# Two decoder blocks on one core: the delta rule's inverse in 32x32 blocks with VectorE's transposes, and gate projections in column tiles

## The reference, cut to what matters

```python
def gdn_mixer(h, w_in, w_conv, a_log, dt_bias, w_onorm, w_out):
    proj = h @ w_in
    qkv, z, beta_logit, a_logit = jnp.split(proj, [3 * GDN_WIDTH, 4 * GDN_WIDTH, 4 * GDN_WIDTH + H], axis=-1)
    qkv = jax.nn.silu(causal_conv(qkv, w_conv))          # 4 taps
    q = q * lax.rsqrt(jnp.sum(q * q, -1) + EPS) / sqrt(d); k = k * lax.rsqrt(jnp.sum(k * k, -1) + EPS)
    ...
# per head and chunk
L = jnp.where(strict, k_beta @ k.T * decay, 0.0)
T = inverse(eye + L)                                     # unit lower triangular
u = T @ v_beta
w = T @ (k_beta * jnp.exp(g_cum))
# scan over chunks
v_new = u_c - w_c @ state
o = qd @ state + qk_c @ v_new
state = state * jnp.exp(gl) + kd.T @ v_new
```

## Time and profile before

| | |
|---|---|
| median of 3 executions | 2048.74 us (2048.35 to 2049.61) |
| the profiled execution | 2048.42 us |
| its span, first to last instruction | 2046.6 us |
| TensorE / VectorE / ScalarE / GpSimd busy | 98% / 72% / 28% / 17% |
| granted TensorE clock, mean | 0.997 |

### The profile page before, as it was taken

The page is one execution under the profiler, slowest core; times in us unless marked ns, Lnnn a source line. Parts: engine busy times, 40 slices in busy tenths (PEclk is TensorE's granted clock), DMA queues, the critical chain, the costliest instruction groups (busy, mean ns, idle before and its releaser), DMA issues.

```text
span 2046.6 us, 31786 instructions
## 1 busy us (share of the span) xinstructions
PE 2015.8 (98%) x12910; PEld 1619.7 (79%) x12910; DVE 1464.6 (72%) x2281; ACT 569.0 (28%) x994; POOL 352.9 (17%) x320
## 2 busy tenths in 40 slices
PE   8999999999999999999999999999999999999999
PEld 6888788887777777777788877777888888888887
DVE  5766666668877777667898887576666778849973
ACT  2000122222544444324883233434310010000000
POOL 2212111111101010012111211111121212222221
PEclk9999999999999999999999999999999999999999
DMA  4323222222211121122222332111223332322232
GB/s 163 112 93 103 80 89 91 93 83 76 84 57 60 63 69 58 64 73 78 68 69 74 119 108 78 62 52 47 78 84 97 100 101 93 104 92 96 101 98 88
DMA packets 53362, 173.73 MB, mean 85 GB/s; under 512 B 6337, under 2 KB 6721, under 8 KB 53089
## 3 DMA queue, kind: packets, MB, share of 16 engines
q1 hardware_dynamic: 48112, 161.67, 23.8%
q10 hardware_dynamic: 5104, 10.03, 1.7%
HBM read 169.51 MB, written 2.16 MB: 84 GB/s over the span
## 4 chain that ended last, share of the span: by engine, by line
PE 45%; DVE 7%; ACT 1%; issue 1%; DVEq 0%; ACTq 0%
PE ps_lin L1818 13%; PE ps_lin L1820 13%; PE ps_lin L1819 13%; PE ps_att L1864 3%; DVE arena L409 2%; PE ps_aux L1864 1%; DVE w_lo L409 1%; ACT arena L1270 1%; DVE arena L415 1%; DVE arena L897 1%; DVE y_lo L409 0%; PE ps_att L1873 0%; DVE sq L409 0%; DVE xw_lo L415 0%; DVE x L409 0%
## 5 line engine op out<-in xcount | busy, mean ns | idle before, releaser
L1818 PE MATMUL ps_lin<-xw_hi,w_hi 128*128 128x512 f32 (+1 forms) x1728 | 698.4, 404 | 0.0
L1820 PE MATMUL ps_lin<-xw_hi,w_lo 128*128 128x512 f32 (+1 forms) x1728 | 674.9, 391 | 0.0
L1819 PE MATMUL ps_lin<-xw_lo,w_hi 128*128 128x512 f32 (+1 forms) x1728 | 674.0, 390 | 0.0
L391 POOL TENSOR_SCALAR w_hi<-raw 128x1024 fp32r<-128x1024 f32 (+5 forms) x312 | 348.3, 1117 | 1678.3 <-PE ps_lin L1820 1554.4
L409 DVE TENSOR_TENSOR w_lo<-raw,w_hi 128x1024 fp32r<-128x1024 f32 (+2 forms) x344 | 381.2, 1111 | 47.9 <-POOL w_hi L391 17.5
L1270 ACT ACTIVATE arena<-arena 128x512 f32<-128x512 f32 (+7 forms) x331 | 206.4, 631 | 742.7 <-DVE arena L409 365.7
L1820 PEld LDWEIGHTS ps_lin<-xw_hi,w_lo 128*128 128x128 f32 (+1 forms) x1728 | 322.7, 187 | 71.6
L1818 PEld LDWEIGHTS ps_lin<-xw_hi,w_hi 128*128 128x128 f32 (+1 forms) x1728 | 323.0, 187 | 68.8 <-issue 4.0
L1819 PEld LDWEIGHTS ps_lin<-xw_lo,w_hi 128*128 128x128 f32 (+1 forms) x1728 | 323.5, 187 | 61.0
L409 DVE TENSOR_TENSOR arena<-ps_lin,rstd 128x512 f32<-128x512 f32 (+2 forms) x213 | 146.7, 689 | 200.5 <-PE ps_lin L1820 185.9
L1818 PE MATMUL ps_lin<-y_hi,w_hi 128*128 128x512 f32 (+1 forms) x544 | 205.4, 378 | 1.2 <-DVE w_lo L409 1.1
(11 more groups left out here) (175 smaller groups left out, 1693.1 us busy)
## 6 DMA issues: line engine op xcount, KB each, us to landing
raw<-in_w_up SPq DMA_DIRECT2D x44, 512.0 KB, 3.3
raw<-in_conv_w_in SPq DMA_DIRECT2D x32, 512.0 KB, 3.3
raw<-in_fox_w_in SPq DMA_DIRECT2D x32, 512.0 KB, 3.3
raw<-in_gdn_w_in SPq DMA_DIRECT2D x32, 512.0 KB, 3.3
raw<-in_w_gate SPq DMA_DIRECT2D x24, 512.0 KB, 3.2
raw<-in_swa_w_in SPq DMA_DIRECT2D x20, 512.0 KB, 3.2
raw<-in_w_ml SPq DMA_DIRECT2D x16, 512.0 KB, 3.3
raw<-in_w_down SPq DMA_DIRECT2D x16, 512.0 KB, 3.5
```

The costliest lines, as they stand in the source:

```text
L391: pool.tensor_scalar(w_whole(n, kc * c)[0], w_raw(n, kc * c), 1.0, 0.0, mult, add).then_inc(s("w_rounded"), 1)
L1818: pe.matmul(o, wh, hi, start=first and k == 0, stop=False)
L1819: pe.matmul(o, wh, lo, start=False, stop=False)
L1820: ins = pe.matmul(o, wl, hi, start=False, stop=last and k == kc - 1)
```

## The change

1. **Gate tiles.** GpSimd skips gate units. VectorE multiplies the raw weights by the norm's weights into `gate_w`, and TensorE multiplies them in plain fp32 with `x` itself, in four column tiles at 0, 32, 64 and 96: for Fox four groups of 128 tokens, for the other two layers two sets of outputs times two halves of 256 tokens. `gate_rows` evacuates each with its own instruction.
2. **The inverse** runs to 32x32 in levels 1 to 4, in `Uc` alone: VectorE copies `V` into `Uc`, and its transpose of 32x32 blocks makes `Ts` from it. The second group loses the product `Y` there, and the first transpose and its copy by ScalarE go. Level 5 joins two 32x32 blocks to 64x64, with 32x32 tiles: `Y` stays only for the upper triangle (`Th`); ScalarE puts the blocks into `Th` and `U`, eight copies. Level 6 is as before.
3. **The fillers** of VectorE come from tables of its own, `DVE_FILL` (before and behind the second group's work of a level) and `DVE_SCAN_FILL`; the four steps ahead of level 1 go to later places. `LEVEL_FILL` of level 3 is 2 instead of 1, in place of the chunk behind the first transpose. Pieces of the last round move by a place.
4. **The first tap** of the convolution is ScalarE's: right behind the evacuation of query and key, three steps later for value.

```diff
-        LEVEL_FILL = (0, 2, 2, 1, 1, 2, 1)
+        LEVEL_FILL = (0, 2, 2, 2, 1, 2, 1)
+        DVE_FILL = (None, (1, 2), (1, 4), (1, 1), (1, 0), (1, 2), (1, 1))
+        DVE_SCAN_FILL = (1, 1, 2, 3)
...
+        def gate_tiles(w, c):
+
+            if w == "fox_w_f":
+                return [(0, c, 32 * j, slice(j * P, (j + 1) * P)) for j in range(NT)]
+            return [(i * c // 2, c // 2, 64 * j + 32 * i, slice(j * T // 2, (j + 1) * T // 2)) for j in range(2) for i in range(2)]
...
+            def gate_rows(t, w, dst, first, release):
+
+                n, c = LAST_UNIT[t], UNITS[LAST_UNIT[t]][4]
+                for col0, m, at, tokens in gate_tiles(w, c):
+                    if col0 == first:
+                        size = tokens.stop - tokens.start
+                        last = tt(dst[:, tokens], ps_lin[at:at + m, t % BANKS, 0:size], rstd[at:at + m, tokens], mult)
...
@@ VectorE, gdn_tile
-                if n:
-                    dve.wait_ge(s("gdn_silu"), n)
-                step(ts(F["t"], F["u"][:, 3:3 + T], col("gdn_w_conv", 3 * 24 + j), mult))
                 for k in range(3):
                     yield
+                    if k == 0:
+                        dve.wait_ge(s("gdn_tap"), n + 1)
...
@@ VectorE, gdn_head
                 U0 = chunks(F["Uc"])
-                for top in (0, HD):
-                    step(tt(U0[top:top + HD], chunks(F["LT"])[top:top + HD, :, top:top + HD], over_chunks(mat("pairs0_ident")[top:top + HD, 0:HD], HD), mult))
-                tt(U0, U0, over_chunks(mat("pairs0_ident")[:, HD:]), add).then_inc(s("gdn_U0"), 1)
+                for at in range(0, P, SQ):
+                    last = tt(U0[at:at + SQ], chunks(F["LT"])[at:at + SQ, :, at:at + SQ], over_chunks(mat("pairs")[at:at + SQ, 0:SQ], SQ), mult)
+                step(last)
+                step(tt(U0, U0, over_chunks(mat("pairs")[:, SQ:2 * SQ]), add))
+                dve.transpose(F["Ts"], F["Uc"]).then_inc(s("gdn_T0"), 1)
...
-                fill(GDN_FILL["U0"])
-                fill(1)
...
-                    fill(1)
+                    fill(DVE_FILL[l][0])
                     if l < 6:
-                        dve.wait_ge(s("gdn_TX"), 5 * h + l)
-                        tt(part(F["Tm"]), part(F["Tm"]), ps_att[:, 1, 0:P].rearrange("p (b d) -> p b d", d=d), add).then_inc(s("gdn_T"), 1)
+                        if l < 5:
+                            dve.wait_ge(s("gdn_XU"), 6 * h + l)
+                            step(dve.tensor_copy(part(F["Uc"], 1), new(ps_att[:, 3, :])))
+                            dve.transpose(F["Ts"], F["Uc"]).then_inc(s("gdn_T"), 1)
+                        else:
+                            dve.wait_ge(s("gdn_TX"), h + 1)
+                            dve.tensor_copy(chunks(F["Th"])[SQ:, :, 0:SQ], chunks(ps_att[SQ:HD, 1, 0:NT * SQ])).then_inc(s("gdn_T"), 1)
...
-                    fill(LEVEL_FILL[l])
+                    fill(DVE_FILL[l][1])
...
-                    fill(1)
+                    fill(DVE_SCAN_FILL[c])
...
@@ ScalarE, gdn_tile
+                def tap():
+
+                    t, n, j = tile_of("gdn_w_in", part * 8 + r), 3 * r + part, part * 8 + r
+                    act.wait_ge(bank_read(t), reads(t))
+                    activation(F["t"], F["u"][:, 3:3 + T], ACT.Copy, scale=col("gdn_w_conv", 3 * 24 + j)).then_inc(s("gdn_tap"), 1)
+
+                late = part == 2 and r
+                if not late:
+                    tap()
...
@@ ScalarE, gdn_head
-                act.wait_ge(s("gdn_U0T"), h + 1)
-                activation(F["Tm"][:, 0:NT * HD], ps_att[:, 2, 0:NT * HD], ACT.Copy).then_inc(s("gdn_T0"), 1)
...
                     if l == 5:
-                        act.wait_ge(s("gdn_U"), 7 * h + 5)
-                        activation(U[0:HD, :, 0:HD], Uc[0:HD], ACT.Copy)
-                        activation(U[HD:, :, HD:], Uc[HD:], ACT.Copy).then_inc(s("gdn_U"), 1)
+                        act.wait_ge(s("gdn_T"), 5 * h + 4)
+                        activation(Th[0:SQ, :, 0:SQ], Ts[0:SQ], ACT.Copy)
+                        activation(Th[SQ:, :, SQ:], Ts[SQ:HD], ACT.Copy).then_inc(s("gdn_Th"), 1)
+                        for at in range(0, P, SQ):
+                            activation(U[at:at + SQ, :, at:at + SQ], Uc[at:at + SQ], ACT.Copy)
+                        act.wait_ge(s("gdn_XU"), 6 * h + l)
+                        activation(U[0:SQ, :, SQ:HD], by_chunk(ps_att[0:SQ, 3, 0:NT * SQ]), ACT.Copy)
+                        activation(U[HD:HD + SQ, :, HD + SQ:], by_chunk(ps_att[HD:HD + SQ, 3, 0:NT * SQ]), ACT.Copy).then_inc(s("gdn_U"), 1)
...
@@ TensorE, project
+                    if weight in GATES:
+                        for col0, m, to, tokens in gate_tiles(weight, c):
+                            ins = pe.matmul(ps_lin[to:to + m, bank, 0:tokens.stop - tokens.start], gate_w[:, k, col0:col0 + m], x[:, k, tokens],
+                                            start=k == 0, stop=k == kc - 1)
...
@@ TensorE, gdn_head
-                for c in range(NT):
-                    for top in (0, HD):
-                        rows = slice(top, top + HD)
-                        last = mm(Z[rows, c * HD:(c + 1) * HD], F["Uc"][rows, c * HD:(c + 1) * HD], mat("ident")[rows, rows])
-                last.then_inc(s("gdn_U0T"), 1)
-                fill(1)
...
-                    if l < 6:
-                        for c, rows, b, off in tiles:
-                            last = mm(to(Y[rows], c), F["Uc"][rows, c * HD + off:c * HD + off + n], half(F["X"][l][rows], c * HD, 0))
-                        last.then_inc(s("gdn_TX"), 1)
-                        for c, rows, b, off in tiles:
-                            last = mm(to(V[rows], c), F["X"][l][rows, c * HD + off:c * HD + off + n], half(F["Uc"][rows], c * HD, 1))
+                    if l < 5:
+                        for rows, at, of, c in squares:
+                            last = mm(to(V[rows], c), F["X"][l][rows, at], half(F["Uc"][rows, at], 1))
+                    elif l == 5:
+                        for a_, b_, at, of in below:
+                            if b_.start == SQ:
+                                last = mm(Y[b_, at], F["Uc"][b_, at], F["X"][l][b_, at])
+                        last.then_inc(s("gdn_TX"), 1)
+                        for a_, b_, at, of in below:
+                            last = mm(V[a_, at], F["X"][l][b_, at], F["Uc"][b_, at])
```

More of the change, by code:

```diff
@@ L59, in stream @@
     residual("fox_w_out")
[L60 removed]
+    tile("gdn_w_gates", 0, ND, 2 * GDN_H, "xw2")
     for h in range(GDN_H):
@@ L106 @@
 WEIGHTS = {u[0]: None for u in UNITS}
+GATES = ("fox_w_f", "gdn_w_gates", "ml_w_gates")
+ROUNDED = [sum(u[0] not in GATES for u in UNITS[:n + 1]) for n in range(len(UNITS))]
 COL_NAMES = [("norm_w", 4 * ND), ("final_norm_w", ND), ("g_mix_2", ND), ("g_mem_2", ND), ("g_ffn_2", ND),
@@ L124 @@
         "window_add", "causal_add"]\
-    + ["before", "pairs0_ident", "pairs1234", "pairs5"]
+    + ["before", "pairs"]
 MAT = {n: i for i, n in enumerate(MATS)}
@@ L687, in _ @@
             third = gdn_tile(0, 2)
-            for _ in range(5):
+            for _ in range(4):
                 next(third)
@@ L1418, in gdn_tile @@
                     root(F["n"], ps_aux[:], "gdn_rn")
-                for _ in range(4):
+                for i in range(4):
                     yield
+                    if i == 1 and late:
+                        tap()
                 use(ACT.Silu)
@@ L2036, in gdn_head @@
                         pe.wait_ge(s("gdn_T"), 5 * h + l - 1)
-                    if l < 6:
-                        for c, rows, b, off in tiles:
-                            last = mm(to(Z[rows], c), F["LT"][rows, c * P + b:c * P + b + n], half(F["Tm"][rows], c * HD, 0))
+                    if l < 5:
+                        for rows, at, of, c in squares:
+                            last = mm(to(Z[rows], c), F["LT"][rows, of], half(F["Ts"][rows, at], 0))
+                    elif l == 5:
+                        for a_, b_, at, of in below:
+                            last = mm(Z[b_, at], F["LT"][a_, of], F["Ts"][a_, at])
+                    else:
+                        pe.wait_ge(s("gdn_Th"), h + 1)
+                        for c in range(NT):
+                            last = mm(Z[HD:, c * HD:(c + 1) * HD], F["LT"][0:HD, c * P + HD:(c + 1) * P], F["Th"][:, c * HD:(c + 1) * HD])
@@ new lines, in gdn_head @@
+                    last.then_inc(s("gdn_XT"), 1)
+                    fill(1)
+                    if l == 5:
+                        pe.wait_ge(s("gdn_QK"), h + 1)
+                    elif l == 6:
+                        pe.wait_ge(s("gdn_U"), 2 * h + 1)
+                    pe.wait_ge(s("gdn_X"), 6 * h + l)
+                    if l < 5:
+                        for rows, at, of, c in squares:
+                            last = mm(to(V[rows], c), F["X"][l][rows, at], half(F["Uc"][rows, at], 1))
+                    elif l == 5:
+                        for a_, b_, at, of in below:
```

(8 more changed lines are left out.)

117 lines of the change are left out of this document (62 added, 55 removed).

## The result

The changed kernel takes 2058.17 us (median of 5 runs, 2056.58 to 2063.92) where the kernel before took 2048.74: ratio 1.0047, 95% interval 1.0036 to 1.0057. It is slower by 0.47%. The prediction was 2040.5, with 0.08 for slower; direction and range were wrong. In the profiled execution the span went from 2046.6 to 2056.4 us.

The account below looks back on a forecast made before the run. It took TensorE, busy 98% of the span, as the bound. Gates 5.0, seven heads 1.5, head 0 0.5 and the last head 1.0 make 8.0 us off 2048.42: about 2040.5, range 2027 to 2049.

Parts of the forecast that it names:

- the serial rival: Gate units: four column tiles run one after the other, +14.7 us, 2063; chance 0.08, with the transpose's upper bound in it.
- GDN: Gate unit at the GDN layer boundary: column tiles were to win 1.6 us.
- mLSTM: Gate unit before the mLSTM tile: nothing is late there, so column tiles were to win 1.8 us.
- TensorE then waits instead, and 1.6 us are won: Fox gate unit: TensorE waits for VectorE's last addition of squares, so 1.6 us are won instead of 3.8.
- TensorE's side of the inverse: Inverse, per head: dropped transposes, shorter second groups and smaller level 5 tiles were to save TensorE 2.86 us.
- lie in its idle time: ScalarE's first taps, 0.63 us each, fit its idle time and free 0.5 us each on VectorE.
- head 0 some 0.5 more: Head 0's round: 0.5 us more won, as its old level 1 waited longer and it has no earlier head's output.
- The new waits: TensorE's added waits for other engines, 2.65 us a head, leaving 0.2 of the 2.86 won.
- the square's chain: Level 2: query's convolution, SiLU and square take about 5.3 us against TensorE's 4.45, so it waits 0.9 us.
- The first rival: Rounds: the filler table hides all waits, -14 to -28 us, 2021 to 2034, rounds near 40.6 us; chance 0.20.
- The prediction's slower case: Gate units: four column tiles run serially, total +14.7 us, 2063; chance 0.08.
- The last head: Last head, without projection fillers and running at latency: 1.0 us was to be won.

Follow-up runs that it names:

- e1: The changed kernel with the first tap of every convolution back on VectorE: 2053.95 us, ratio 1.003 to the kernel before.
- e5: The changed kernel with GpSimd rounding only 64 of 1024 columns of each GDN projection weight tile (output not the reference's): 2052.58 us, ratio 1.0019 to the kernel before.
- e6: The changed kernel with level 5's four copies of the inverse's diagonal blocks moved from ScalarE to VectorE: 2057.49 us, ratio 1.0043 to the kernel before.
- e8: The changed kernel with only query's normalisation moved ahead of level 6's product on VectorE: 2057.35 us, ratio 1.0041 to the kernel before.
- o2: The changed kernel with another VectorE filler table, output split and value weight halves moved, round 0's value first tap on VectorE: 2022.92 us, ratio 0.9873 to the kernel before.
- e2: The changed kernel with only round 0 reordered, value's first tap behind the gate rows' exponentials, product be before VectorE's taps: 2056.12 us, ratio 1.004 to the kernel before.
- e9: The changed kernel with all first taps on VectorE and its fillers in step with TensorE's, without the table: 2043.33 us, ratio 0.9973 to the kernel before.
- e3: The kernel before with the gate tiles alone in column tiles: 2046.07 us, ratio 0.9989 to the kernel before.

## Why the prediction was wrong

**Gate tiles.** The concurrency was right (the serial rival falls: 56 matmuls in 1.72 us), and so were GDN (1.6 against 1.54) and mLSTM (1.8 against 1.85). The Trainium skill (TensorEngine Tiling (Array Packing), Restrictions) says only that column tiling disables Fast Weight Load; no run here shows whether that was in use before. What I had drawn from it, that nothing would be won, is not borne out by GDN's and mLSTM's rows. Fox was wrong in its step "TensorE then waits instead, and 1.6 us are won": the additions that it waits for were themselves stretched by a rounding that comes sooner, by 0.78 us, and the wait was followed by half clock, 1.6 to 1.7 us more. Without the half clock 0.6 would have been won (seven profiles). A wait was priced at its length alone.

**TensorE's side of the inverse.** 2.86 us predicted, 3.05 measured; second groups take 0.37 (785.38 to 785.75), transposes 0.31 on VectorE. Right.

**Round 0 and head 0.** The sentence that ScalarE's first taps "lie in its idle time" failed, and with it the sum, which has no term for round 0. I looked at ScalarE in a steady round only. In round 0 the tap waits for an evacuation and stands ahead of the gate rows' exponentials. Cost 5.63 us, half clock included; e1 gives 5.46 of it back. The step "head 0 some 0.5 more" failed too: with the 0.2 of a round it makes 0.7 us won, and head 0's own round lost 1.28, of it 0.93 for the first transpose behind the memsets.

**The new waits.** 2.65 predicted, 4.37 measured, which turns -0.2 a round into +1.3. This is the largest failed step: 10.06 us lost in seven heads, where 2.0 were to be won. By place, predicted and measured: level 2 0.9 and 1.36; level 5 with the place ahead of it 0.65 and 0.65; behind level 6 0.3 and 0.89; head's end 0.8 and 1.47. The walk had the right places and got the square's chain nearly right (TensorE stands at 788.59, 0.79 us late). It lacked three things:
- the weight halves, which are fillers too and move with the table, and for which each tile's first projection waits (0.57 us in level 2, 0.57 at the scan's end);
- GpSimd's rounding, which starts whenever TensorE finishes a tile, wherever VectorE then is. It took 1.29 us a round (e5), part of the first item with it. The kernel before had it too, where nobody waited: a weight half at 803.07 took 0.91 us instead of 0.69;
- the buffer that query's normalisation frees for the root: I counted ScalarE's copies and took 0.3, with a second chain of the same length beside them (e6, e8).

The first rival, that the table hides all, fell for this table (44.8, not 40.6 us). Rounds of 40.6 us exist all the same: o2 reaches them with another table. The prediction's slower case was another mechanism, column tiles one after the other, and that one didn't happen.

**The last head** gained more than the 1.0 that I gave: from its first product to the sum of squares behind it 35.11 us became 32.54, and up to the mLSTM gates 1.3 more. The latter is no gain of the change. It falls in one place, between the last head and the mLSTM gates, where TensorE waits 1.88 us in both kernels, before and after:

```profile
973.69 2.35 PE L1864 MATMUL ps_att<-arena 64*128 64x128 f32 x16 [1.88 <-DVE arena L409]
```

```profile
986.59 1.79 PE L1928 MATMUL ps_att<-arena 64*128 64x128 f32 x16 [1.88 <-DVE arena L423]
```

In the profile before the granted clock was 0.76 from 972 to 979 us, in that after 1.00 from 985 to 992. This luck hid 1.3 us of loss, a little less than the half clock at Fox added.

**What stays open.** The half clock. It followed waits of TensorE of 3.54 us (after) and 2.05 us (e2) in round 0, of 1.92 us at Fox and of 1.31 us in e9's rounds, and yet stayed away behind the Fox boundary in 7 of the 13 profiles with the new gate tiles, o2 among them, and behind the same waits of two of e9's rounds. I can say what it cost where it came, not when it comes.

## What to carry to other kernels

When a queue of fillers is shifted, list every operation in it and ask for each who waits for it, also the dull ones (weight halves, a buffer given back); and walk the first round as well as a steady one. Two waits that end together hide each other: when removing one does nothing, look at what ended the idle time then, and remove both. A change that shortens TensorE's work is worth what the order of the other engines lets through: the same small matmuls gave seven rounds of 314 us with one order of VectorE's fillers and of 284 with another, against 304 before.

## What the runs showed of the hardware

- A VectorE operation with two operands in SBUF takes 1.53 us instead of 0.69 when a GpSimd rounding of 1.24 us is under way (814.75), and ends 0.53 us behind it (814.51 + 1.24 = 815.75, 816.28), most of its own length. That is a wait and no slower pace: the 14 weight halves of 512 columns that start inside a rounding in the two profiles, before and after, start 0.24 to 0.68 us into it, and every one ends 0.53 or 0.54 us behind it, 1.52 us long the earliest and 0.91 the latest. An evacuation with one operand in PSUM keeps its 0.68 us beside a rounding (o2, 761.43). The Trainium skill (SBUF — State Buffer, Who interferes with whom) says that a VectorE instruction with two SBUF inputs contends with a GpSimd instruction that reads SBUF, and that the later one blocks until the first is done; by that rule, the trace agrees, and e5 shows it by taking the rounding away.
- After TensorE had waited 1.3 to 3.5 us, the granted clock could fall to 0.50: five (e3) to eight projections at Fox start 0.43 us apart instead of 0.23. It cost 1.6 us at Fox, 1.3 in the kernel before behind 973.69 and 1.1 to 1.5 in a round of e9, on top of the wait. Waits of the same length (1.92, 1.88, 1.31 us) passed without it in other profiles or rounds.
- Four fp32 column tiles of eight columns start 7 ns apart, and the next four follow 0.216 us after the first for 256 tokens each (e3's 64 matmuls: 3.64 us with their tail), 0.11 us for 128 tokens (Fox).
